# Four dense feed-forwards of a two-block network: the remainder of the down slabs by a second, adding transfer

## The reference, cut to what matters

```
def swiglu(h, w_gate, w_up, w_down):
    return (jax.nn.silu(h @ w_gate) * (h @ w_up)) @ w_down

x = x + swiglu(rmsnorm(x, norm_ffn[0]), ffn_w_gate[0], ffn_w_up[0], ffn_w_down[0])        # after the convolution mixer
x = x + moe_swiglu(rmsnorm(x, norm_ffn[1]), ...)                                          # after latent attention
for i in range(2):
    x = x + 0.5 * swiglu_2(rms_norm(x, ffn1_norm[i]), ffn1_w_gate[i], ffn1_w_up[i], ffn1_w_down[i])
    x = x + (moba_mixer, mamba2_mixer)[i](rms_norm(x, mix_norm[i]), ...)
    x = x + 0.5 * swiglu_2(rms_norm(x, ffn2_norm[i]), ffn2_w_gate[i], ffn2_w_up[i], ffn2_w_down[i])
```

## Time and profile before

| | |
|---|---|
| Median of the runs | 2086.11 us |
| Profiled execution, span from first to last instruction | 2084.0 us |
| TensorE (PE) busy | 2046.0 us, 98% |
| VectorE (DVE) busy | 1409.6 us, 68% |
| ScalarE (ACT) busy | 1198.0 us, 57% |
| GpSimd (POOL) busy | 93.9 us, 5% |
| Read from device memory | 461.11 MB, mean 224 GB/s over the span with what is written |

### The profile page before, as it was taken

How to read it: one execution, slowest core, us unless ns; L and a number is a source line. 1 busy time by engine, 2 the same in 40 slices (tenths; PEclk the granted TensorE clock), 3 DMA queues, 4 the chain that set the end, 5 groups by cost and what they waited for, 6 DMA issues and landing times.

```text
span 2084.0 us, 27770 instructions
## 1 busy us (share of the span) xinstructions
PE 2046.0 (98%) x10189; PEld 1713.0 (82%) x10189; DVE 1409.6 (68%) x1529; ACT 1198.0 (57%) x1374; POOL 93.9 (5%) x140
## 2 busy tenths in 40 slices
PE   9999999999999999999999999999999999999999
PEld 9988887778878878787788877888888899888887
DVE  6655457698888988889444685445555579785444
ACT  4454458677777777776344565444444465874442
POOL 1010001000000000010100010000000000220000
PEclk9999999999999999999999999999999999999999
DMA  8555434389999999998555443555455455445551
GB/s 305 187 183 185 180 140 145 122 326 362 361 362 370 357 362 351 367 384 339 183 185 194 160 164 145 185 195 184 178 184 181 147 180 194 162 152 182 190 192 41
DMA packets 68267, 467.11 MB, mean 224 GB/s; under 512 B 7776, under 2 KB 8176, under 8 KB 13520
## 3 DMA queue, kind: packets, MB, share of 16 engines
q1 hardware_dynamic: 63616, 455.24, 59.0%
q10 hardware_dynamic: 3536, 8.10, 1.2%
q0 software_dynamic: 1024, 2.56, 0.5%
HBM read 461.11 MB, written 4.75 MB: 224 GB/s over the span
## 4 chain that ended last, share of the span: by engine, by line
PE 84%; DVE 6%; ACT 5%; issue 3%; DVEq 1%; ACTq 0%; POOL 0%; POOLq 0%
PE gu L2146 15%; PE gu L2148 15%; PE gu L2147 15%; PE acc L2146 9%; PE acc L2148 9%; PE acc L2147 9%; DVE wlo L1303 3%; ACT whi L710 2%; PE acc L2242 2%; PE acc L2244 2%; PE acc L2243 2%; PE tp L2256 1%; PE tp L2175 1%; PE acc L2696 1%; PE tp L2728 1%
## 5 line engine op out<-in xcount | busy, mean ns | idle before, releaser
L1303 DVE TENSOR_TENSOR wlo<-raw,whi 128x2048 fp32r<-128x2048 f32 (+2 forms) x435 | 987.1, 2272 | 365.6 <-ACT whi L710 365.2
L710 ACT ACTIVATE whi<-raw 128x2048 fp32r<-128x2048 f32 (+1 forms) x436 | 827.4, 1899 | 214.5 <-PE acc L2148 165.9
L2146 PE MATMUL gu<-whi,actA_hi 128*128 128x512 f32 (+1 forms) x1448 | 575.4, 397 | 3.6 <-DVE actA_lo L1324 1.5
L2147 PE MATMUL gu<-wlo,actA_hi 128*128 128x512 f32 (+1 forms) x1448 | 563.0, 389 | 1.3 <-issue 1.3
L2148 PE MATMUL gu<-whi,actA_lo 128*128 128x512 f32 (+1 forms) x1448 | 564.0, 389 | 0.0
L2146 PEld LDWEIGHTS gu<-whi,actA_hi 128*128 128x128 f32 x1448 | 272.0, 188 | 59.8 <-issue 5.3
L2148 PEld LDWEIGHTS gu<-whi,actA_lo 128*128 128x128 f32 x1448 | 271.7, 188 | 59.1 <-issue 1.5
L2147 PEld LDWEIGHTS gu<-wlo,actA_hi 128*128 128x128 f32 x1448 | 272.4, 188 | 52.0
L2146 PE MATMUL acc<-whi,hT_hi 128*128 128x512 f32 x656 | 256.6, 391 | 4.4 <-DVE wlo L1303 4.1
L2148 PE MATMUL acc<-whi,hT_lo 128*128 128x512 f32 x656 | 255.6, 390 | 0.0
L2147 PE MATMUL acc<-wlo,hT_hi 128*128 128x512 f32 x656 | 255.4, 389 | 0.0
(11 more groups left out here) (448 smaller groups left out, 2257.2 us busy)
## 6 DMA issues: line engine op xcount, KB each, us to landing
raw<-in_slabs SPq DMA_DIRECT2D x427, 1024.0 KB, 4.9
y_rows<-big ACTq DMA_DIRECT2D x7, 512.0 KB, 7.4
raw<-in_slabs SPq DMA_DIRECT2D x4, 576.0 KB, 3.7
hT_hi<-cum_rows ACTq DMA_DIRECT2D x8, 256.0 KB, 3.1
hT_lo<-cum_rows ACTq DMA_DIRECT2D x8, 256.0 KB, 4.3
raw<-in_slabs SPq DMA_DIRECT2D x2, 768.0 KB, 4.1
raw<-in_slabs SPq DMA_DIRECT2D x2, 640.0 KB, 3.9
x<-in_x SPq DMA_DIRECT2D x2, 512.0 KB, 4.8
```

The costliest lines, as they stand in the source:

```text
L710: act.activation(whi[:, n0 % SPLIT, 0:w], raw[:, n0 % RAW, 0:w], ACT.Copy).then_inc(slab_hi, 1)
L1303: dve.tensor_tensor(wlo[:, n0 % SPLIT, 0:w], raw[:, n0 % RAW, 0:w], whi[:, n0 % SPLIT, 0:w].bitcast(F32), ALU.subtract).then_inc(slab_spli ...
L2146: pe.matmul(o, xh, wh, start=start, stop=False)
L2147: pe.matmul(o, xh, wl, start=False, stop=False)
```

## The change

In four dense feed-forwards the remainder of the 11 down slabs is made in another way, 44 slabs in all. VectorE's subtraction is left out for them. ScalarE reads the loaded slab twice: it first writes the negated, rounded slab into `wlo`, and then the rounded slab into `whi` as before. When the first is done, GpSimd starts a transfer that reads the same slab once more from device memory and adds it, element by element, onto what is in `wlo`: `-round(slab) + slab`, which is the remainder. TensorE waits for that transfer's semaphore ahead of the first product of the down slab. VectorE keeps a copy of one element per partition in the place of the subtraction, which waits for both of ScalarE's writes and then increments `slab_split`, so that `raw` is free for the next load.

```diff
+        passed = sb("passed", [P, 4])
+        down_neg = sem("down_neg")
+        down_lo = [sem("down_lo%d" % n) for n in range(2)]
...
+        def by_transfer(f):
+            return f.kind == "ffn" and f.gates is None and not f.opened
+        def downs_before(f):
+            return sum(g.C for g in stages_used[:stages_used.index(f)] if by_transfer(g))
+        def down_of(f, k):
+            return ffn_kind(f, k, 0)[1] if by_transfer(f) and ffn_kind(f, k, 0)[0] == "down" else None
...
+                if by_transfer(f):                                   # GpSimd
+                    for c in range(f.C):
+                        k = 3 * f.C - 1 if c == f.C - 1 else 3 * c + 4
+                        n = downs_before(f) + c + 1
+                        pool.wait_ge(down_neg, n)
+                        pool.dma_start(wlo[:, (f.s0 + k) % SPLIT, :], a["slabs"][f.s0 + k],
+                                       accum_op=ALU.add).then_inc(down_lo[(n - 1) % 2], 16)
...
+            def negated(f, k, i):                                    # ScalarE
+                n0 = f.s0 + k
+                act.wait_ge(raw_full[n0 % RAW], 16 * (n0 // RAW + 1) + 16 * i)
+                act.wait_ge(slab_used, n0 + 1 + RAW * i)
+                act.activation(wlo[:, n0 % SPLIT, :], raw[:, n0 % RAW, :], ACT.Copy, scale=-1.0).then_inc(down_neg, 1)
...
+                    if k + 2 < 3 * C and down_of(f, k + 2) is not None:
+                        negated(f, k + 2, i)
                     ahead(f.s0, k, i, C // 2 * ex)
...
+            def remainder_by_transfer(f, k, i):                      # VectorE
+                dve.wait_ge(slab_hi, f.s0 + k + 1 + RAW * i)
+                dve.wait_ge(down_neg, downs_before(f) + down_of(f, k) + 1 + 2 * i)
+                dve.tensor_copy(passed[:, down_of(f, k) % 4:down_of(f, k) % 4 + 1], n_half[:, 0:1]).then_inc(slab_split, 1)
...
-                    if not at_end:
+                    if k + 2 < 3 * C and down_of(f, k + 2) is not None:
+                        remainder_by_transfer(f, k + 2, i)
+                    elif not at_end:
                         ahead(f.s0, k, i, C // 2 * ex)
...
+                        if by_transfer(f):                           # TensorE, down slab
+                            n = downs_before(f) + c
+                            pe.wait_ge(down_lo[n % 2], 16 * (n // 2 + 1 + i))
```

## The result

The changed kernel takes 2135.57 us (2 runs, 2135.23 to 2135.92) against 2086.11 us: a ratio of 1.0238, 95% interval 1.0222 to 1.0255. It is slower, as forecast, but by 49.5 us where 104 were forecast, and about half of the 49.5 us (24 to 29, by two experiments) come from a cause that the prediction did not contain.

A forecast was written before the change was run, and what follows sets the result against it. TensorE, busy for 98% of the span, was taken as the bound. 2084 us plus 101 of late landings plus 4 at stage ends made 2189, 2191 as median of runs, forecast as 2190 us; range 2084 to 2340 us.

The forecast's parts named there:

- the forecast's own case: TensorE stalls of 1 to 5 us ahead of down slabs, 2130 to 2306 us; chance 0.43.
- rival A: Adding transfer lands inside 9.0 us, no stall: 2086 us, up to 2127 with stalls under 0.95 us; chance 0.33.
- the forecast's border of "slower": Whole kernel: under 2% (42 us) counts as no change, up to 2128 us; chance of slower 0.65.
- I take nothing: Removing 44 VectorE subtractions, 101 us, in the changed stages: gain between nothing and 1.15 us, taken as nothing.
- the transfer's own time: Engine time of one adding transfer onto wlo: two reads where a load has one, 5.8 us.
- term 1: At down slabs, one load's 2.9 us delays landing to 11.3 us, 2.3 us late; 44 times, 101 us.
- the window: From the negated slab's write to the down slab's first weight load: 9.0 us; only later landing costs time.
- term 2: At each stage's end two adding transfers 6.4 us apart share engines with two loads: 1 us more, 4 stages.
- the sign: In the profile after, the distance between TensorE's products was to stay at 0.227 us.

The follow-up runs named there:

- e2: The whole change with the buffer passed declared behind all other buffers, not behind wlo: 2111.57 us, ratio 1.0121 to the kernel before.
- e9: The change without each stage's last down slab, passed behind all others, whi products issued ahead of the wait and wlo products after: 2085.87 us, ratio 1.0000.
- e4: The change with the second transfer overwriting wlo with the slab instead of adding (values wrong, for time alone): 2114.74 us, ratio 1.0142.
- e1: The kernel before with only an unused buffer of 16 declared bytes per partition behind wlo: 2114.78 us, ratio 1.0141.
- e7: The kernel before with an unused buffer of 16 declared bytes between hT_lo and h_tok: 2087.46 us, ratio 1.0007.
- e12: The kernel before with the buffer qk_ss (128 bytes per partition) moved from further behind to behind wlo: 2112.89 us, ratio 1.0130.

## Why the prediction was right in direction and wrong in size

**Right in direction, in part by luck.** The measured 2135.57 us lie inside the 2130 to 2306 us of the forecast's own case, but not by its stall of 1 to 5 us. With the buffers back in their places the whole change takes 2111.57 us (e2): that is rival A's "up to 2127 with a stall under 0.95 us", which had a chance of 0.33, and the waits in the loops, at most 0.7 us each, are rival A's too. The placement, which no rival held, lifted the time over 2128 us, the forecast's border of "slower".

**Right: what bounds the stages, and that nothing is gained.** "I take nothing" for 44 subtractions less is shown by e9. ScalarE's writes, the copies and GpSimd's place in the order cost nothing (e4 against e1: 2114.74 and 2114.78).

**Right: the transfer's own time.** "An adding transfer reads the slab and also what is in `wlo`, two reads where a load has one, so I take 5.8 us": 5.7 us of the 16 engines, against 3.1 without adding. Landing without loads beside it was 0.7 + 1.9 + 5.8 = 8.4 by that sum and 7.8 to 8.1 in the last pair. The Trainium skill ("Collectives: The Full Stack", section "The bandwidth ceiling") says of the reduce-scatter of a ring of cores that it runs at half the speed of the plain exchange because the adding needs two source reads; it states this for rings only, and the 5.7 against 3.1 us of this local transfer agree. The fit of the Trainium skill ("DMA: Bandwidth & Descriptors", section "Anatomy of one DMA — SWDGE (gpsimd) path") gives an estimate of 4.4 us for a slab, which is near the 5.2 us of the plain transfer and half of the adding one's 9.2 us.

**Wrong, term 1: sharing with the load.** The step that failed is "at least one slab load (2.9 us) goes through the same engines", which put the load's whole time ahead of the landing: 11.3 us. The loop showed 9.2 us, 1.1 to 1.4 more than the transfer alone. Which of the two gets how much of the engines was not measured by itself; the numbers say only that the load's 2.9 us did not all fall into the transfer's time. So the lateness against 9.0 us was 0.2 us and not 2.3, and since nothing is paid below zero, small errors in the landing were large ones in the price: 4.5 us for the 40 slabs and not 92. Two small terms were missing as well. GpSimd starts the transfer 0.3 us after ScalarE's write has ended, so with the buffers of before the wait is 0.3 us a slab, 12.3 us for the 40 (e2); in the change the longer products widen the window by 0.25 us and hide most of that. And behind a wait the second product follows the first after 0.33 us and not 0.23: 2.2 us in the change. Rival A's condition, landing inside 9.0 us, was missed by 0.2 us.

**Wrong, term 2: the pair at a stage's end.** I gave 2.3 + 1 us to each of four. Three of them waited 2.8 to 4.2 us (9.9 in all) and the fourth not at all, as the loads had ended. Behind the three came what I had no term for: 5.4 us, by the sum of the lengthened distances, of products at the lower clock, where every row before showed the upper one.

**Wrong, and the largest: a term that was not in the sum.** I read the product distance as 0.227 us and asked only whether it could shrink with less traffic. That the line `passed = sb("passed", [P, 4])` moves every activation buffer against the weights (by 32 bytes) stood in the diff. It makes the 512-column products 2.4% longer in all stages, 29 us by e1's runs and 29.7 us between the spans of e1 and before (2113.7 and 2084.0). The sum for the spans is then 29.7 + 4.5 + 9.9 + 5.4 + 2.2 = 51.7 us, against 50.2 measured; small waits elsewhere in the kernel are shorter by the difference. Without the placement my forecast of 104 us would have stood against 26, four times too much.

That is also why the time alone misleads. A landing of 10.1 us, 1.1 us late 44 times, would have given 48 us, nearly what was measured, and the sign "the distance between products still 0.227 us", which I had set down, is what told the two apart.

## What to carry to other kernels

When a kernel is bound by one engine, compare that engine's pitch in a stage the change does not touch before explaining anything in the stage it does; a new buffer in the middle of the allocations is a change of its own, so declare it last. A late transfer costs only what exceeds its window, so compute the window and the landing to a tenth of a us where they are within 1 us of each other; and where a wait belongs to one operand of several, issue the products of the others first: 16 products ahead of the wait took away all 14 us that were left (e9).

## What the runs showed of the hardware that I had not expected

- The start of the activations relative to the start of the weight buffers sets the distance of 512-column products: 0.2265 us with the buffers of before, 0.2266 at 256 bytes more, 0.2313 to 0.2322 us at 32, 64 and 128 bytes more. For the 256-column products of the table, which stream the activations past loaded weights, it goes the other way: 0.120 against 0.116 to 0.119 us. The weight loads (PEld) of the 512-column products take 188 ns in either. Why is open.
- TensorE's lower clock was granted for 3.4, 3.4 and 6.8 us at the ends of three stages of the change, by the clock's own records, with waits of 2.9, 2.8 and 4.2 us in otherwise full stages. The first two stretches begin when the products run again or 0.5 us later, the third 2.0 us before its wait has ended. In e2 it came once, with the wait of 3.2 us (at 1675 us), and not with those of 2.1 and 2.5 us. The length of the wait alone does not decide: in e7 (at 982 us) and in e12 (at 993 us) 3.4 us at the lower clock came with a wait of 1.5 us, and the kernel before has the same wait at the full clock.
- A 1024 KB transfer that adds in place takes 5.7 us of all 16 engines and lands after 7.8 to 8.1 us alone, 9.2 us (the median) in the loops, where three slabs are loaded in about 17.4 us, up to 13.2 us where another adding transfer lies ahead; the same without adding takes 3.1 us and lands after 5.2 us. GpSimd is busy for 0.86 us with starting the one and 0.53 us with the other.
